# A hybrid decoder step: the tail of each attention head interleaved with the next stage's first projection

## What is computed

```
q, k, v, z_gla, a_lo, gates = split(rms_norm(x) @ w_in)
g  = log_sigmoid(a_lo @ w_a2 + b_a) / 16            # per head, from wa2
o, S_new = gla_chunked(q, k, v, g, S0)              # causal, with a state per head
o  = o * rsqrt(mean(o * o) + eps) * gla_norm_g      # norm per head
yB = (o * silu(z_gla)) @ w_gla_o
y  = sigmoid(gA) * yA + sigmoid(gB) * yB            # gB: the gate stage
```

## Time and profile before

| | us |
|---|---|
| median of 3 runs | 1186.61 (1181.58 to 1188.57) |
| the profiled execution | 1186.15 |
| its span, first to last instruction | 1184.4 |
| PE busy | 1149.3 (97%) |
| DVE busy | 540.2 (46%) |
| ACT busy | 423.5 (36%) |
| POOL busy | 199.2 (17%) |
| mean granted clock of TensorE | 0.988 |

### The profile page before, as it was taken

How to read it: one execution, slowest core, us unless ns; L and a number is a source line. 1 busy time by engine, 2 the same in 40 slices (tenths; PEclk the granted TensorE clock), 3 DMA queues, 4 the chain that set the end, 5 groups by cost and what they waited for, 6 DMA issues and landing times.

```text
span 1184.4 us, 17796 instructions
## 1 busy us (share of the span) xinstructions
PE 1149.3 (97%) x6888; PEld 1108.4 (94%) x6888; DVE 540.2 (46%) x711; ACT 423.5 (36%) x557; POOL 199.2 (17%) x128
## 2 busy tenths in 40 slices
PE   5899999999999999999999999999999999999997
PEld 5899999999999999999999999999989999999886
DVE  5777777775000001662395357438534002444332
ACT  5555555554111112542543453345434111122211
POOL 3511111111212120210112011111202121120000
PEclk8999999999999999998999999999999999999999
DMA  6211111111211222210311131031002103432331
GB/s 210 65 41 49 48 40 40 40 36 37 91 55 54 72 75 64 68 37 18 112 35 35 35 95 35 18 96 52 18 18 80 49 18 110 154 117 90 107 106 54
DMA packets 95488, 76.18 MB, mean 64 GB/s; under 512 B 3928, under 2 KB 88792, under 8 KB 95464
## 3 DMA queue, kind: packets, MB, share of 16 engines
q1 hardware_dynamic: 84444, 61.59, 17.5%
q10 hardware_dynamic: 11020, 14.26, 3.5%
HBM read 62.04 MB, written 13.80 MB: 64 GB/s over the span
## 4 chain that ended last, share of the span: by engine, by line
PE 88%; issue 6%; DVE 3%; ACT 2%; DMA 0%; DVEq 0%; ACTq 0%
PE ps L455 26%; PE ps L456 25%; PE ps L457 25%; PE ps L590 2%; PE ps L653 1%; PE ps L632 1%; PE ps L624 1%; PE ps L634 1%; PE ps L617 1%; DVE xcs L1197 1%; PE ps L672 1%; ACT xcs L870 1%; PE ps L561 1%; DVE xc L1189 1%; PE ps L581 1%
## 5 line engine op out<-in xcount | busy, mean ns | idle before, releaser
L455 PE MATMUL ps<-xn,whi 128*128 128x364 f32 x1344 | 451.9, 336 | 1.7 <-DVE xn L1124 1.5
L456 PE MATMUL ps<-xn,whi 128*128 128x364 f32 x1344 | 443.1, 330 | 0.0
L457 PE MATMUL ps<-xn,wlo 128*128 128x364 f32 x1344 | 442.7, 329 | 0.0
L423 POOL TENSOR_TENSOR wlo<-raw,whi 128x1024 fp32r<-128x1024 f32 x72 | 180.9, 2513 | 860.6 <-ACT whi L817 860.6
L455 PEld LDWEIGHTS ps<-xn,whi 128*128 128x128 f32 x1344 | 254.0, 189 | 6.1 <-issue 2.5
L456 PEld LDWEIGHTS ps<-xn,whi 128*128 128x128 f32 x1344 | 254.2, 189 | 0.2
L457 PEld LDWEIGHTS ps<-xn,wlo 128*128 128x128 f32 x1344 | 253.7, 189 | 0.0
L817 ACT ACTIVATE whi<-raw 128x1024 fp32r<-128x1024 f32 x72 | 76.0, 1056 | 151.6 <-PE ps L457 85.9
L456 PE MATMUL ps<-act_s,whi 128*128 128x364 f32 x384 | 126.2, 329 | 0.0
L455 PE MATMUL ps<-act_s,whi 128*128 128x364 f32 x384 | 126.2, 329 | 0.0
L457 PE MATMUL ps<-act_s,wlo 128*128 128x364 f32 x384 | 126.1, 329 | 0.0
(11 more groups left out here) (230 smaller groups left out, 1367.2 us busy)
## 6 DMA issues: line engine op xcount, KB each, us to landing
raw<-in_w_in SPq DMA_DIRECT2D x56, 512.0 KB, 3.8
branch_a<-keep ACTq DMA_DIRECT2D x8, 546.0 KB, 2.8
mal<-branch_a SPq DMA_DIRECT2D x8, 544.0 KB, 4.6
xt<-in_x_prompt SPq DMA_DIRECT2D x8, 512.0 KB, 6.8
raw<-in_w_lru_o SPq DMA_DIRECT2D x8, 512.0 KB, 3.6
st<-in_state_gla ACTq DMA_DIRECT2D x4, 1024.0 KB, 5.5
out<-st ACTq DMA_DIRECT2D x4, 1024.0 KB, 4.7
raw<-in_w_gla_o SPq DMA_DIRECT2D x8, 512.0 KB, 5.7
```

Source lines behind the costliest of these rows:

```text
L423: pool.tensor_tensor(wlo[:, c % 2], raw[:, c % 2], whi[:, c % 2].bitcast(F32), ALU.subtract).then_inc(s["lo_ok"], 1)
L455: pe.matmul(dst, wh, mh, start=first, stop=False)
L456: pe.matmul(dst, wh, ml, start=False, stop=False)
L457: return pe.matmul(dst, wl, mh, start=False, stop=last)
```

## The change

On PE, job 0 leaves the top of the head. For head 0 it stands ahead of the loop. For the later heads it is "job 6" of the head before (and behind head 3 it is the first job of the gate stage): its 24 products are spread over the tail, and the order of the tail becomes Os, mean squares, outer products. All of job 5 is done ahead of the outputs. The head now begins with g0 and g1, half a piece of job 1, and g2.

On ACT the Tanh of job 5 moves ahead of the output copies, the q copy goes between the drains of g1 and g2, `hi` of jobs 7, 8 and 9 and the load of the sample state move, the rest of the norm goes to `inv` (the second half of `qk`) instead of `kt`. The load of `wa2` moves to SP, its split to the tail of the head before. The last head is written out apart from the loop. On DVE the SiLU product and both additions of squares come ahead of the state updates.

```diff
+    steps += [(f"nrm{j}", "act") for j in range(PIECES)]
     steps += [(f"sKV{n}", "dve") for n in range(NSEQ // 2)]
-    steps += [(f"nrm{j}", "act") for j in range(PIECES)]
...
@@ SP, head loop, behind the load of job 0 @@
+                    if j == 0:
+                        sp.wait_ge(s["wa2_lo"], h + ONE)
+                        for r in range(6):
+                            sp.dma_start(wa2_raw[...], t["w_a2"][...]).then_inc(s["wa2_in"], 16)
...
@@ PE, ahead of the head loop @@
+            pe.wait_ge(s["lo_ok"], N_GLA + 1)
+            piece(N_GLA, bankA, xn, 0)
+            piece(N_GLA, bankA, xn, 1)
+            pe.wait_ge(s["alo_ok"], PIECES)
+            piece(N_GLA, bankA, xn, 2).then_inc(s["job_done"], 1)
+            pe.wait_ge(s["tails_ok"], 2)
+            pe.wait_ge(s["ma_ok"], KT + ONE)
...
@@ PE, in sample_output @@
-                    between = iter(range(2, KT - 1))
+                    between = iter(range(KT))
-                            if q in (2, 5) or (q == NSEQ - 1 and d == 0):
-                                part(5, bankB, 2, range(k, k + 1))
+                            if q % 2 == 1 and (d == 0 or q < NSEQ - 1):
+                                part(6, bankA, 0, range(k, k + 1))
...
@@ PE, top of a head @@
-                start_job(0)
-                part(0, bankA, 0)
-                part(0, bankA, 1)
-                part(0, bankA, 2)
                 pe.wait_ge(s["wa2_lo"], h + (ONE + 1))
                 gate(0)
                 gate(1)
                 start_job(1)
-                part(1, bankB, 0)
+                pe.wait_ge(s["zg_silu"], 2 * h + ONE)
+                part(1, bankB, 0, EARLY)
                 gate(2)
+                part(1, bankB, 0, LATE)
...
@@ PE, tail of a head @@
-                part(5, bankB, 2, range(2))
+                part(5, bankB, 2)
...
+                start_job(6)
+                pe.wait_ge(s["zg_silu"], 2 * h + (ONE + 1))
                 c_step("Os", sample_output)
+                part(6, bankA, 0, range(KT - 1, KT))
+                pe.wait_ge(s["sq_sum"], 2 * h + 1)
+                mean_square(0)
+                part(6, bankA, 1, range(0, 2))
+                mean_square(1)
+                part(6, bankA, 1, range(2, 6))
+                pe.wait_ge(s["sq_sum"], 2 * (h + 1))
+                mean_square(2)
+                part(6, bankA, 1, range(6, KT))
                 sample_outer(0)
+                part(6, bankA, 2, range(0, 1))
                 sample_outer(1)
-                part(5, bankB, 2, range(KT - 1, KT))
+                part(6, bankA, 2, range(1, 3))
                 sample_outer(2)
+                part(6, bankA, 2, range(3, 5))
                 sample_outer(3)
-                pe.wait_ge(s["sq_sum"], 2 * (h + 1))
-                for j in range(PIECES):
-                    mean_square(j)
+                part(6, bankA, 2, range(5, KT))
...
@@ PE, gate stage @@
+            job(0, N_GB + 1, bankB, xn)
-            with pe.Fori(0, KT // 2) as i:
+            with pe.Fori(1, KT // 2) as i:
...
@@ ACT, head @@
-                act.wait_ge(s["wa2_lo"], h + ONE)
-                for r in range(6):
-                    act.dma_start(wa2_raw[...], t["w_a2"][...]).then_inc(s["wa2_in"], 16)
-                job_at(0)
-                act.activation(p3(qb[:, :]), slot3(bankA), ACT.Copy, ...)
-                hi(3 * h, N_GLA + 2)
                 act.wait_ge(s["og_ok"], 2 * h + ONE)
                 for j in range(PIECES):
                     full(f"g{j}")
                     act.activation(gb[...], ps[...], ACT.Identity, ...)
+                    if j == 1:
+                        job_at(0)
+                        act.activation(p3(qb[:, :]), slot3(bankA), ACT.Copy, ...)
...
                 act.activation(dd[:, :], dd[:, :], ACT.Ln, bias=1.0).then_inc(s["g_ln"], 1)
+                hi(3 * h, N_GLA + 2)
...
                 squares(slice(0, SEQ))
+                hi(3 * h, N_GLA + 7)
                 full("Os")
...
+                if not last:
+                    wa2_high(h + 1)
+                act.wait_ge(s["sq_sum"], 2 * h + 2)
...
@@ DVE, tail @@
+                dve.scalar_tensor_tensor(p3(keep[:, 2 * h + 1, :]), p3(vT[:, :]), 1.0, slot3(bankB), ALU.add, ALU.mult)
                 add_squares(0)
+                add_squares(1)
                 for n in range(NSEQ // 2):
-                    if n == 2:
-                        add_squares(1)
                     full(f"sKV{n}")
...
-                dve.scalar_tensor_tensor(p3(keep[:, 2 * h + 1, :]), p3(vT[:, :]), 1.0, slot3(bankB), ALU.add, ALU.mult)
+                if not last:
+                    wa2_low(h + 1)
                 dve.wait_ge(s["n_rstd"], h + 1)
```

More of the change, by code:

```diff
@@ L215, in build @@
         oo = [gb, kb]
+        inv = qk[:, 1, :]
         ring = [dd, kt]
@@ L376, in _ @@
                     load(6 * h + (N_GLA + j), (N_GLA + j) % 2, w_in[:, :, bass.ds(h * step + col, P)])
+                    if j == 0:
+                        sp.wait_ge(s["wa2_lo"], h + ONE)
+                        sp.sem_inc(s["sp_passed"], 1)
+                        for r in range(6):
+                            sp.dma_start(wa2_raw[r * RANK:(r + 1) * RANK, :], t["w_a2"][0][:, bass.ds(h * P, P)]).then_inc(s["wa2_in"], 16)
             with sp.Fori(0, KT // 2) as i:
@@ L689, in _ @@
                 start_job(1)
-                pe.wait_ge(s["ma_ok"], KT + ONE)
-                part(1, bankB, 0)
+                pe.wait_ge(s["zg_silu"], 2 * h + ONE)
+                part(1, bankB, 0, EARLY)
                 gate(2)
+                part(1, bankB, 0, LATE)
                 part(1, bankB, 1)
@@ L929, in _, with wa2_high, act_head @@
                 act.dma_start(dst, trow[r0:r0 + nr, :]).then_inc(s["tails_out"], 16)
-            with act.Fori(0, HEADS) as h:
+            def wa2_high(h):
+                act.wait_ge(s["wa2_in"], 96 * h + 96)
+                act.activation(wa2[:, :], wa2_raw[:, :], ACT.Copy).then_inc(s["wa2_hi"], 1)
+            def act_head(h, last):
                 def job_at(c):
@@ L976, in _ @@
                                    bias=vec[:, h, R_BA:R_BA + 1]).then_inc(s["c_act"], 1)
+                    if j == 1:
+                        job_at(0)
+                        act.activation(p3(qb[:, :]), slot3(bankA), ACT.Copy, scale=float(DK) ** -0.5).then_inc(s["q_ok"], 1)
                 act.wait_ge(*emptied(h, "g2"))
@@ L983, in _ @@
                 act.activation(dd[:, :], dd[:, :], ACT.Ln, bias=1.0).then_inc(s["g_ln"], 1)
+                hi(3 * h, N_GLA + 2)
                 job_at(1)
                 act.activation(p3(kb[:, :]), slot3(bankB), ACT.Copy).then_inc(s["k_ok"], 1)
-                hi(3 * h, N_GLA + 3)
                 level_exp(0)
                 level_exp(1)
+                hi(3 * h, N_GLA + 3)
+                act.wait_ge(s["st0_out"], 16 * h + ONE)
+                act.dma_start(st0[:, :, :], t["state_gla"][0].rearrange("b h p v -> h p b v")[h]).then_inc(s["st0_in"], 16)
                 level_exp(2)
@@ L1028, in _ @@
                 ins.then_inc(s["smp_hi"], 1)
+                job_at(5)
+                act.wait_ge(s["zg_silu"], 2 * h + (ONE + 1))
+                act.activation(p3(vT[:, :]), slot3(bankB), ACT.Tanh, scale=0.5).then_inc(s["zg_tanh"], 1)
                 for g in range(2):
@@ L1044, in _ @@
                 squares(slice(SEQ, TOK))
-                job_at(5)
-                act.wait_ge(s["zg_silu"], 2 * h + (ONE + 1))
-                act.activation(p3(vT[:, :]), slot3(bankB), ACT.Tanh, scale=0.5).then_inc(s["zg_tanh"], 1)
+                if not last:
+                    wa2_high(h + 1)
+                act.wait_ge(s["sq_sum"], 2 * h + 2)
                 for j in range(PIECES):
                     full(f"nrm{j}")
-                    act.activation(kt[:, j * PIECE:(j + 1) * PIECE], ps[:, bank(f"nrm{j}"), 0:PIECE], ACT.Ln,
+                    act.activation(inv[:, j * PIECE:(j + 1) * PIECE], ps[:, bank(f"nrm{j}"), 0:PIECE], ACT.Ln,
                                    bias=ssum[:, 31:32]).then_inc(s["c_act"], 1)
-                hi(3 * h, N_GLA + 7)
                 act.wait_ge(*emptied(h, "nrm2"))
-                act.activation(kt[:, :], kt[:, :], ACT.Exp, scale=-0.5).then_inc(s["n_rstd"], 1)
+                act.activation(inv[:, :], inv[:, :], ACT.Exp, scale=-0.5).then_inc(s["n_rstd"], 1)
                 act.wait_ge(*emptied(h, "KV3"))
@@ L1059, in _ @@
                 act.dma_start(out[7][0].rearrange("b h p v -> h p b v")[h], st0[:, :, :]).then_inc(s["st0_out"], 16)
+            wa2_high(0)
+            with act.Fori(0, HEADS - 1) as h:
+                act_head(h, False)
+            act_head(HEADS - 1, True)
             act.wait_ge(s["og_ok"], 2 * HEADS + ONE)
@@ L1262, in _, with wa2_low, dve_head @@
             dve.wait_ge(s["ma_out"], 16 * KT)
-            with dve.Fori(0, HEADS) as h:
+            def wa2_low(h):
+                dve.wait_ge(s["wa2_hi"], h + 1)
```

(10 more changed lines are left out.)

15 lines of the change are left out of this document (3 added, 12 removed).

## The result

| | before | changed |
|---|---|---|
| median of 7 runs, us | 1185.07 | 1198.05 |
| lowest to highest | 1181.58 to 1190.49 | 1196.93 to 1199.01 |
| the profiled execution | 1186.15 | 1197.61 |
| its span | 1184.4 | 1195.9 |

The changed kernel takes 1.0105 times as long (95% interval 1.0087 to 1.0123). The forecast was 1203, the range 1194 to 1210. It is slower, as forecast, but by 11.5 us between the profiled executions where 17 were summed.

What follows compares the result with a forecast made beforehand. PE's own instruction list, with PE busy 97% of the span, was taken to bound the kernel. 1186.15 + 0 - 5.8 + 10.5 + 6.3 + 0 + 6.2 = 1203.35, about 1203 us; range 1194 to 1210.

Steps and rivals of the forecast that it cites:

- Part 1: PE's work per head: 24 products move into the tail, interleaving cost and filled gaps together 0 us (-0.5 to +0.7).
- changes between kinds make 0.3 to 0.9: In the tail, PE's extra switches between kinds of matmul and two more sample-output products cost 0.3 to 0.9 us.
- Part 2: Tails of heads 0 and 1: denser products keep the full clock, -5.8 us (bounds -5.8 and 0).
- Part 3: PE waits at g2 behind heads 0, 1 and 2 for og_ok's chain: 3.5 us each, +10.5 (+7.5 to +13.5).
- Part 4: Gate stage behind head 3: PE waits for the third gate job's weights, +6.3 us (+5.5 to +7.3).
- Part 5: Other moved work, such as job 8's hi behind Ln: 0 in the sum, that hi 0 to 1.0 us per head.
- Part 6: Low clock behind the new waits: 1.4 us for each of three, 2.0 at the gate stage, +6.2.
- the rule on idle gaps: Leave no idle gaps between matmul bursts if the clock is to hold; so each new wait costs more than its length.
- The waits come, but the clock holds: Waits at g2 and the gate stage come, without low clock behind them: 1198 us, chance 0.20.
- Half the wait: At g2 and the gate stage, og_ok comes 1.8 us sooner than summed, no low clock: 1190 us, chance 0.08.
- the tail keeps its low clock too: The tails stay at low clock and the waits come with theirs: 1209 us, chance 0.14.
- faster: The chain to g0's drain is covered, no waits at g2 or gate stage, clock gain only: 1180.4 us, chance 0.08.

Runs made afterwards that it cites:

- both edits: Changed kernel with the gate drained to kt without og_ok, and ACT's high part and first Tanh earlier at the gate stage: 1174.80 us, rerun 1174.57.
- the three runs above: Five or no products in the sample output of the kernel with both edits: 1176.21, 1181.65 us; seven instead of five in the kernel before: 1182.89.
- the sparse spacing: Kernel with both edits, but five products in the sample output and three behind it: median 1176.21 us, 0.9912 of before.
- the bare sample output: Kernel with both edits, but no product in the sample output and all eight behind it: median 1181.65 us, 0.9970 of before.

## Why the prediction was right, point by point

**The bound.** PE sets the time before and after. What the change gains and loses is all on PE: a wait, a low clock, or time between matmuls.

**Part 1, the work on PE: mis-sized.** It was 0 per head, bounds -0.5 and +0.7. In head 0 of the changed kernel the outputs start at 548.25 and g0 at 575.33: 27.08 us with 24 products (12.0), so 15.1 for the rest. Head 2 of before took 19.28 with six products (3.0): 16.3. That is **-1.2** per head, -4.8 in all, outside my bounds. The terms: sample output 8.57 to 563.60 with eight products, 4.6 for the rest, as before (4.5). Mean squares 5.83 to 569.43 with eight products: 1.83, where before they took 2.44 with their wait. Outer products 4.38 to 573.81 with five: 1.88, where before they took 2.55. The step that failed is "changes between kinds make 0.3 to 0.9": they cost nothing that the rows show. The 0.15 us said for each product in the sample output are 0.01 (4.57 for the rest with eight products, 4.5 with five and with none). An outer product follows a product at no cost (0.17 to 0.18 us between their starts, as any two). And a mean square costs less among products than bare:

```profile
565.20 0.77 PE L685 MATMUL ps<-qk,ones 128*128 128x364 f32 x2
...
567.81 0.77 PE L685 MATMUL ps<-qk,ones 128*128 128x364 f32 x2
```

From the one to the other it is 2.61 us, and without the four products between them 0.61, where a bare one took 0.70 (a third of 781.16 - 779.05). What the filled gaps save is 0.6 and 0.7, not 0.3 to 0.6 together. The kernel with both edits bears this out without waits or low clock: its heads are 104.0 us long against 105.4.

**Part 2, the clock in the tail: right** in the profiled execution, -5.8 us, and shown by the three runs above to be due to the products in the sample output. The low bound of 0 was needed less than thought: no execution of the kernel with both edits lay above 1175.6. What the single profile of before could not show is that its own share varies: 1180.6 to 1190.5 us over all its executions, so that the median gives back less than 5.8. The three runs shown first spread by 7.0 us, and that should have been read as this.

**Part 3, the wait at g2: right in place, cause and size.** Chain: last outer product issued at 573.81, updates end at 574.89 (S + 1.08; 1.07 was said), `og_ok` at 580.27 (S + 6.46; 6.45), g2 at 581.20 (S + 7.39; 7.35). PE stood there at 577.78 (S + 3.97; 3.83). The waits were 3.42 between starts in heads 1 and 2 and a little less in head 3: 10.1 against 10.5. Removing the wait for `og_ok` ahead of the drains removes it all.

**Part 4, the gate stage: right.** Idle 6.00 on the row, 6.2 between the starts, against 6.3; the run that reorders ACT shows it alone.

**Part 5: the 0 was right, the margin was not seen.** The weights of job 2 cost nothing in the changed kernel, though in head 1 PE takes them only 0.13 us after they are ready (591.47 and 591.34). The text treated the chain behind g2 as a matter of 0.3 us; with g2 later it is 1.8 us per head. It was a bound that hid behind another, and the prediction did not say so. The 0.3 us at 1017.95, in the stage on `w_gla_o`, were in no part of it: ACT's high part waited there for the load of the weights.

**Part 6, the clock behind the waits: right in kind, a little too dear.** Two of three waits of 3.3 us and the long one were followed by half clock. From 689.31 the products are 0.91 apart instead of 0.50, three of them, and the fourth is slow in part. From the start of g2 to the end of four products it is 3.82 us in head 2 (688.85 to 692.67) and 3.81 in head 3, against 2.28 in head 1, where the clock held: 1.5 us lost in each. In the gate stage, with five products and a bit, it is 2.5. Together 5.6 against 6.2. By the rule on idle gaps that the prediction named (the Trainium skill, "TensorE: Matmul & The Clock Gate", table of goals), each of these four waits puts the full clock at risk; the trace agrees at three of them, and the 3.26 us in head 1 went by without a fall.

The sum with what was measured: 1186.15 - 4.8 - 5.8 + 10.1 + 6.2 + 0.3 + 5.6 = 1197.75 (the 0.3 is the wait at 1017.95); the profiled execution had 1197.61. The 5.7 us between it and the forecast of 1203.35 are the 4.8 of Part 1 and small shares of Parts 3 and 6.

**The rivals.** "The waits come, but the clock holds" gave 1198, the time that was measured, but by other terms: the clock did fall, and Part 1's gain made up for it. A total alone would have spoken for the wrong case; the windows tell them apart. "Half the wait" is excluded by the three waits of 3.1 to 3.3 us, "the tail keeps its low clock too" by the windows at 1.00, and "faster" by the waits themselves.

## What to carry to other kernels

When filler work is moved off a stage to thicken another, ask what its old place covered: each chain that ended under it (here DVE's normalisation up to a bank's drain, and ACT's splits up to the next weights) must be followed to its last consumer, and the one behind it too, since letting PE arrive later merely uncovered the next. Repair such a wait by starting its chain earlier (a buffer of its own, the needed instruction first in the queue), not by shifting its consumer. And where executions of one kernel spread by more than the measurement should, look at the granted clock in the stretches of narrow matmuls: in this kernel seven products among them, 0.95 us apart, instead of five, 1.2 us apart, took 2 us off the median and nearly all of the spread.

## What was not expected of the hardware

- The same code has its clock lowered in some executions and not in others: with the sparse spacing 1174.1 and 1183.8 us came from one kernel. With the dense one the spread was 1.5 us at most (0.6 and 1.5 with both edits, 1.1 in the kernel before with denser products).
- The clock fell to half in stretches in which PE was never idle (with the bare sample output a mean of 0.57 from 556 to 564 us, PE busy all 8.00 us). Yet in the changed kernel it held through one idle time of 3.26 us between dense products and fell behind two others of 3.27 and 3.09. Why it held there is open.
- After pauses of only 1.26 and 1.79 us some 8 us apart (g2 half a piece later) it fell all the same, in two heads out of the three that have both pauses.
- A product of three matmuls of 364 columns, set among matmuls of 8 columns, cost 0.01 us more than in a row of its like.
